# A shared sample search and denser key logits in a one-core hybrid decoder step

## The reference

```
x = x + 0.5 * swiglu(rms_norm(x)) ; h = rms_norm(x)
u, q, k, v, qi, ki, wi, gates = h @ w_in, split, normed, rotated
sample scores: sum over index heads of wi * relu(qi . ki) over 4096 cached + 8 new keys
idx = top 256 keys per query; logits = q . k[idx]; att = softmax(logits) @ v[idx]
x = x + (gate_c * conv(u) + gate_a * (att @ w_aout)) @ w_o
x = x + 0.5 * swiglu(rms_norm(x))
```

## Time and profile before

| | |
|---|---|
| median of the runs | 1529.44 us |
| profiled execution | 1525.64 us |
| its span | 1523.2 us |
| PE busy | 1428.6 us (94%) |
| VectorE busy | 1070.5 us (70%) |
| POOL busy | 587.3 us (39%) |
| ACT busy | 512.5 us (34%) |
| granted clock, mean | 0.98 |

### The profile page before, as it was taken

The page is one execution under the profiler, slowest core; times in us unless marked ns, Lnnn a source line. Parts: engine busy times, 40 slices in busy tenths (PEclk is TensorE's granted clock), DMA queues, the critical chain, the costliest instruction groups (busy, mean ns, idle before and its releaser), DMA issues. The chain is left out here.

```text
span 1523.2 us, 20730 instructions
## 1 busy us (share of the span) xinstructions
PE 1428.6 (94%) x8219; PEld 1123.1 (74%) x8219; DVE 1070.5 (70%) x1640; ACT 512.5 (34%) x776; POOL 587.3 (39%) x415
## 2 busy tenths in 40 slices
PE   4998999989989999999889898999998999999998
PEld 2333688867878875436666565679998999999998
DVE  1257798998826898999996997667669756664221
ACT  2333422123632231121112233453365444453111
POOL 2000564444338755544335675223203553420000
PEclk8998999999999999999999999999999999999999
DMA  9995363222227888879438875532422223312222
GB/s 345 391 380 205 99 98 105 89 81 69 81 77 246 286 258 291 279 215 314 152 102 272 265 229 175 170 132 75 134 87 69 87 83 109 99 50 74 84 87 87
DMA packets 156929, 248.75 MB, mean 163 GB/s; under 512 B 11965, under 2 KB 104909, under 8 KB 156571
## 3 DMA queue, kind: packets, MB, share of 16 engines
q1 hardware_dynamic: 131742, 164.22, 33.3%
q0 software_dynamic: 23104, 76.16, 15.9%
q10 hardware_dynamic: 1989, 7.07, 1.2%
HBM read 237.58 MB, written 10.20 MB: 163 GB/s over the span
## 5 line engine op out<-in xcount | busy, mean ns | idle before, releaser
L2749 POOL TENSOR_TENSOR w_lo<-w_raw,w_hi 128x1024 fp32r<-128x1024 f32 x65 | 168.2, 2589 | 243.9 <-ACT w_hi L1331 243.7
L695 PE MATMUL ps<-bh,wqr 128*128 128x288 f32 x936 | 205.3, 295 | 4.2 <-DVE wqr L1922 2.0
L1331 ACT ACTIVATE w_hi<-w_raw 128x1024 fp32r<-128x1024 f32 (+1 forms) x88 | 91.4, 1039 | 251.9 <-PE ps L646 181.4
L2816 POOL DMA_INDIRECT kv<-cache_v,idxT x128 | 136.6, 1068 | 100.1 <-PE ps L1109 50.6
L2804 POOL DMA_INDIRECT kv<-cache_k,idxT x128 | 138.5, 1082 | 86.1 <-DVE kprod L2442 53.9
L695 PEld LDWEIGHTS ps<-bh,wqr 128*128 128x128 f32 x936 | 155.5, 188 | 5.1 <-DVE wqr L1922 3.9
L646 PE MATMUL ps<-h_hi,w_hi 128*128 128x512 f32 x352 | 138.6, 394 | 1.2 <-POOL w_lo L2749 1.2
L646 PE MATMUL ps<-h_hi,w_lo 128*128 128x512 f32 x352 | 137.1, 390 | 0.0
L646 PE MATMUL ps<-h_lo,w_hi 128*128 128x512 f32 x352 | 137.0, 389 | 0.0
L711 PE MATMUL ps<-a_hi,wqr 128*128 128x288 f32 x704 | 122.6, 295 | 0.0
L1094 PE MATMUL ps<-h,wn 128*128 128x288 f32 x448 | 114.3, 412 | 8.8 <-DVE U_p L2269 3.7
(11 more groups left out here) (499 smaller groups left out, 3156.8 us busy)
## 6 DMA issues: line engine op xcount, KB each, us to landing
w_raw<-w_ffn_in SPq DMA_DIRECT2D x56, 512.0 KB, 12.4
wq<-w_ffn_in SPq DMA_DIRECT2D x40, 512.0 KB, 3.6
wn<-w_in SPq DMA_DIRECT2D x36, 512.0 KB
qb<-q_scratch SPq DMA_DIRECT2D x64, 256.0 KB
ring<-w_ffn_in SPq DMA_DIRECT2D x28, 512.0 KB
w_raw<-w_ffn_out SPq DMA_DIRECT2D x24, 512.0 KB, 9.6
wq<-w_ffn_out SPq DMA_DIRECT2D x20, 512.0 KB
ring<-w_ffn_out SPq DMA_DIRECT2D x14, 512.0 KB
```

Source lines behind the costliest of these rows:

```text
L695: mm = pe.matmul(ps[:, bank + m, 0:HALF], w[:, k, m * P:(m + 1) * P], b[:, j, k, :], start=(j in (0, 1, 5) and k == 0 and fst), stop=(k == ...
L1331: act.activation(w_hi[:, slot, 0:n], w_raw[:, slot, 0:n], ACT.Copy).then_inc(S_("hi_ready"), 1)
L2749: pool.tensor_tensor(w_lo[:, slot, 0:n], w_raw[:, slot, 0:n], w_hi[:, slot, 0:n].bitcast(F32), ALU.subtract)\
L2816: pool.indirect_dma_start(kv[:, V_SLOT[j % 3] + a // 2, a % 2, :], None, rows[1], bass.IndirectOffsetOnAxis(ap=idxT[:, j % 2, t:t + 1], ax ...
```

## The change

It has four parts. **The search is shared:** VectorE counts the first 1184 columns of `S`, and ACT counts the other 928 by Sign with an accumulator (`tally`, between its high parts, L1595 of the new kernel). VectorE joins the two counts with one more instruction, and a new function `next_up` follows the 31 steps: one more count over all columns and an addition of one where needed. **The work behind it stands earlier on PE:** the ranks are turned after unit 25 (28 before), the ends spread after 26, the one-hot products follow units 31 to 38, the rows unit 39 (43 before). **Key logits:** places begin at 41 (45 before), with two in every odd unit from 47 to 57; 34 tokens instead of 26 have a place ahead of `UA`. **Low parts:** those of units 45, 48, 51 and 54 are made by VectorE.

```
+        CUT = 1184
-        ROWS_AT = 43
+        ROWS_AT = 39
-        KEYS = [v for v in range(45, 59)] + ...
+        KEYS = [v for v in range(41, 59) for n in range(1 + (v >= 46 and v % 2))] + [v for v in range(59, 67)] + [67, 67]
+        SHARED = (45, 48, 51, 54)
-            return max(KEYS[n - KV] + 3, gather_after(n - 1) + 1)
+            return max(KEYS[n - KV] + 3, gather_after(n - 1) + (n % 3 > 0))
 # PE
-                        if (i, j) == (5, 0):
+                        if (i, j) == (4, 1):
                             ranks_turn()
-                        if (i, j) == (5, 1):
+                        if (i, j) == (4, 2):
                             ends_spread()
-                        if (6, 2) <= (i, j) <= (7, 3):
-                            onehots(4 * i + j - 26)
+                        if (5, 3) <= (i, j) <= (7, 2):
+                            onehots(4 * i + j - 23)
 # ACT
+            def tally(n):
+                for r in range(counted[0], counted[0] + n):
+                    act.wait_ge(S_("choice_step"), r + 2)
+                    act.activation(EQ[:, CUT:], S[:, CUT:], ACT.Sign, scale=-1.0, bias=ismall[:, 2:3].bitcast(F32), accum_out=cnts[:, 1:2]).then_inc(S_("scored"), 1)
...
+                    if i > i0 and i < 4:
+                        high_part(i - 1)
+                        tally(1)
                     hi(b + 2)
                     if i == 0:
                         qk_sample_evac()
+                    if i < 4:
+                        tally(2)
+                    hi(b + 3)
                     act.wait_ge(S_("unit_used"), b + 4)
                     (silu)
-                    hi(b + 3)
+                    if i < 4:
+                        tally(2)
                     hi(b + 4)
+                    if i < 4:
+                        tally(1)
                 for n in range(1, 9 if t < 2 else 8):
                     hi(out_unit(t) + n)
+                    if t == 0 and n < 6:
+                        tally((1, 2, 2, 1, 2)[n - 1])
 # VectorE, a step of the search
-                    lk(count(x_.bitcast(F32), ALU.is_ge, cnts[:, 0:1]))
-                    both(cnts[:, 1:2], cnts[:, 0:1])
+                    link(dve.tensor_scalar(EQ[:, 0:CUT], S[:, 0:CUT], x_.bitcast(F32), 0.0, ALU.is_ge, ALU.add, accum_out=cnts[:, 0:1]))
+                    dve.wait_ge(S_("scored"), 16 + i + 1)
+                    settle()
+                    lk(dve.scalar_tensor_tensor(out=cnts[:, 2:3], in0=cnts[:, 1:2], scalar=-0.5, in1=cnts[:, 0:1], op0=ALU.mult, op1=ALU.add))
+                    both(cnts[:, 3:4], cnts[:, 2:3])
...
-            search(27, 29)
-            out_add(0, 2)
-            search(29, 31)
-            out_add(0, 3)
+            search(28, 31)
+            out_add(0, 1)
+            next_up()
             lk(dve.tensor_tensor(x_, cur, flip, ALU.bitwise_xor))
...
             (cnts[:, 5:6], L2338)
+            out_add(0, 2)
             (selection, L2339, L2340)
+            out_add(0, 3)
             (second scan, L2343)
...
             onehot(0)
+            prod(5)
+            onehot(1)
             low_part(5)
-            onehot(1)
             onehot(2)
 # VectorE, the keys' loop; POOL, the loop of the low parts
+                if v + 2 in SHARED:
+                    dve.wait_ge(S_("lo_ready"), v + 4)
+                if in_unit(10) <= v + 2 < UA or v + 2 in SHARED:
                     split_lo(v + 2, v % 2, usize(v + 2))
...
+                if u - 1 in SHARED:
+                    pool.wait_ge(S_("lo_ready"), u + 2)
+                if u not in SHARED:
+                    lo(u)
```

More of the change, by code:

```diff
@@ L1532, in _ @@
                 rb = (relu_a, relu_b, relu_c, relu_d)[n // 2 % 4]
-                act.activation(rb[:, n % 2, :, :], ps[:, 2 * (n % 2):2 * (n % 2) + 2, :], ACT.Relu).then_inc(S_("relu_ready"), 1)
+                act.activation(rb[:, n % 2, :, :], ps[:, 2 * (n % 2):2 * (n % 2) + 2, :], ACT.Relu).then_inc(S_("scored"), 1)
                 if n == 6:
@@ L1598, in _ @@
                         qk_sample_evac()
-                    if i > i0:
+                    if i > i0 and i >= 4:
                         high_part(i - 1)
[L1601 to L1604, removed]
+                    if i < 4:
+                        tally(2)
+                    if i in (6, 7):
+                        weigh(4 * i - 22)
+                    hi(b + 3)
                     act.wait_ge(S_("unit_used"), b + 4)
@@ L1619, in _ @@
                         high_part(i1 - 1)
-                    if t == 1 and n in (1, 3):
-                        weigh(6 + n // 2)
+                    if t == 0 and n < 6:
+                        tally((1, 2, 2, 1, 2)[n - 1])
                     if t == 2 and n in (4, 6, 7):
@@ L2355, in _ @@
             dve.wait_ge(S_("ranks_taken"), 4)
-            low_part(4)
             lk(dve.tensor_scalar(tmpi[:, :, :], RTi[:, :, :], 4, None, ALU.arith_shift_right))
@@ L2370, in _ @@
                 if c == 0:
-                    prod(5)
+                    low_part(4)
             dve.sem_inc(S_("ranks_taken"), 1)
@@ L2402, in _ @@
             onehot(0)
+            prod(5)
+            onehot(1)
             low_part(5)
-            onehot(1)
             onehot(2)
-            prod(6)
-            onehot(3)
-            low_part(6)
-            onehot(4)
-            onehot(5)
             dve.wait_ge(S_("ends_done"), 2)
@@ L2416, in _ @@
             settle()
-            prod(7)
+            onehot(3)
+            onehot(4)
+            onehot(5)
+            prod(6)
             take_own(0)
-            low_part(7)
             onehot(6)
+            low_part(6)
             onehot(7)
@@ L2424, in _ @@
                               nb[:, :].unsqueeze(1).to_broadcast([NS, H, NS]), ALU.add).then_inc(S_("X_ready"), 1)
-            out_add(1, 0)
             take_own(1)
@@ L2458, in _ @@
                     prod(10)
-                if in_unit(10) <= v + 2 < UA:
+                if v + 2 in SHARED:
+                    dve.wait_ge(S_("lo_ready"), v + 4)
+                if in_unit(10) <= v + 2 < UA or v + 2 in SHARED:
                     split_lo(v + 2, v % 2, usize(v + 2))
-                for cg in range(1, 4):
-                    if v == max(out_end(1, cg), ROWS_AT + 1):
+                if v == ROWS_AT + 1:
+                    prod(7)
+                    low_part(7)
+                for cg in range(4):
+                    if v == out_end(1, cg):
                         out_add(1, cg)
```

70 lines of the change are left out of this document (41 added, 29 removed).

## The result

The changed kernel takes 1544.39 us (median of 7 runs, 1541.86 to 1552.73); the kernel before took 1528.35 in the same session. The ratio is 1.0116, 95% interval 1.0088 to 1.0143: slower. The forecast was 1541, slower, with a range up to 1551. The profiled execution has a span of 1540.3 us against 1523.2, 17.1 more. The total came out near the forecast, in part by luck: two of its terms were wrong by 7 and by 3.5 us, in opposite directions.

A forecast was written before the change was run, and what follows sets the result against it. PE was taken as the bound nearly everywhere. Terms 2.8 + 5.5 + 2.9 + 2.5 - 2.0 = +11.7 on 1525.64 gave 1537.3, and with 3.8 for the median 1541 us; range 1521 to 1551, the forecast case's own 1531 to 1548.

The forecast's parts named there:

- The first tallies: Units 3 and 4: ACT's high parts stand behind tallies, 1.4 us later at each; +2.8, bounds -0.9 to +4.5.
- ACT's stream: Rival: tallies of 1.5 us instead of 1.15 delay units, 1548; chance 0.12 together with none of the saving.
- The shared port: Two-input VectorE instructions and POOL low parts exclude each other; a unit's first join waits 1.4 us, its second does not.
- The search's end and the ranks: Units 24 to 25: search ends at 286.9, ranks at 325.5, PE waits 12.7 for 7.2; +5.5, bounds -2.5 to +11.
- a shift of 2.8: The lateness from the first tallies, +2.8 us, carried to later units, so unit 25 ends at 312.8.
- my signs of being wrong: `CUM` ends less than 8 us after unit 25, or over 6 us of PE's waits go behind unit 67.
- The one-hots: One-hot products: waits of 3.0 at the first and 5.8 at the third, none at the seventh; +2.9, bounds -6 to +6.
- The keys: Units 46 to 58: VectorE and POOL both full, a late VectorE low part near unit 58; +2.5, bounds 0 and +8.
- Behind unit 67: VectorE has 8 logits fewer, the 0.76 wait and most of the 1.80 go; -2.0, bounds -6.2 and 0.
- The rivals: Short chain 1521, 0.17; VectorE's work behind unit 67 1534, 0.16; ACT's stream 1548 or none of the saving, 0.12.
- The short chain: Rival: joins, `next_up` and copies meet no low part, ranks come at 315.7; -8, 1521; chance 0.17.
- The search could end where it did: Rival: VectorE's half plus waiting costs what was saved, ranks some 12 us later; over 1548; chance 0.12 with ACT's stream.

The follow-up runs named there:

- onehot_order: The changed kernel with `low_part(5)` behind the third set of one-hots, not ahead of it; ratio to the kernel before 1.0023.
- paced_gathers: The changed kernel with POOL, behind its low parts, starting each key token's gather no earlier than its logit's unit; ratio to the kernel before 1.0028, chip 13.
- combined: Kernel before plus shared search, units 3 and 4 high parts ahead of first tallies, one-tensor-operand join and XOR, `out_add(0, 2)` and `out_add(0, 3)` earlier; ratio 0.9964.
- after_again: The changed kernel as it is, run again on chip 4; ratio to the kernel before 1.0060.

## Why the forecast was right, and where not

The total is 5.4 us over the forecast. Of that 1.5 stands ahead of unit 0, where nothing changed; 7.0 too little for the keys and 3.5 too much for ranks and one-hots offset each other in part. That is luck, and the mechanism of the largest term, the keys, was not the one worked out.

*The first tallies (+2.8, bounds -0.9 to +4.5).* Right: 0.95 and 1.2 at units 3 and 4, where 1.4 each was worked out, and 0.9 at unit 8, which was not foreseen. A tally takes 1.07 and 0.19 us (1.15 between starts was expected), so ACT's stream did not break.

*The shared port.* Right in kind, shown by the two forms of the join. Of 31 joins only six were held over a microsecond, not one in two: I laid them over the low parts by one unit's pattern.

*The search's end and the ranks (+5.5).* The chain was right: counted from the same unit the search ended within 0.2 us of the 286.9 worked out, and PE waited for `xT` at unit 24 (4.5, forecast 5.6) and then for `CUM`. The ranks were mis-sized: `CUM` was ready at 324.08, with the start of units 4.7 later, so 3.3 earlier than 325.5 at a shift of 2.8. Of these 2.7 are `next_up`, which took 4.4 us (289.90 to 294.27) and not 7.1: none of its small ones was held. The one held was the XOR behind it (L2361, 2.05), which I had counted as free; in return of the two copies only one was held (2.21), and from that XOR on the chain took 29.8 for 30.2. PE's wait was 2.2, not 7.1, while unit 24 cost 2.6 us of slow matmuls, a term missing from my sum here though I had it for the one-hots; nor had I seen that the slow turned ranks of before (3.63 us, now 1.97) would go. By unit 30, which has ranks and ends behind it in both kernels, the stage had cost 1.0 us, not 5.5. One of my signs of being wrong was that `CUM` ends less than 8 us after unit 25. It ended 2.1 after it; without the waits ahead, as the sum reckoned (314.7), 9.4 after it. The sign was badly put, for the forecast itself left only 7.1 there.

*The one-hots (+2.9).* Right in both waits: 2.77 for 3.0 and 5.70 for 5.8, and none at the seventh. From unit 30 to 47 the cost was 4.0, since the products behind both waits were slow (3.39 and 3.60 for 1.96) and I had 1.0 for one. onehot_order showed the reason given for the third, `low_part(5)` behind ACT's high part. This one place is worth 8 us at unit 47.

*The keys (+2.5, bounds 0 and +8).* Wrong, outside its own bounds: 9.5. The step that failed is what comes late there. I took a late low part of VectorE and priced that. The low part was late because ACT had PE's signal for unit 57 only 9.0 us after the unit's end; VectorE stood idle for 7.1 us before it made it. The wait of 4.97 and 1.7 of slow matmuls in unit 59 are 6.7 of the 9.5; the other 2.8, and the 3.4 of paced_gathers, are near the 2.5. Nothing in the sum stood for such a signal, though the kernel before shows one, 1.5 us late with 0.5 us to spare. Of the six traces with 26 tokens ahead of unit 67 and no pacing only combined waited there (3.86); of the four with 34 tokens three waited 3.4 to 5.0 and one 0.7. But two of the six and none of the four are of chip 13, where nothing waits; so the traces make it likely that density favours the wait, no pair of runs on one chip shows it, and combined shows that it is not needed for it. Why the signal comes late beside a run of gathers, and on one chip and not on another, stays open, and so does whether taking the profile has a part in it.

*Behind unit 67 (-2.0).* The number is right, the reason only partly. PE is 19.1 us behind the kernel before at 573 and 13.5 at 783 (the waits answering to the earlier trace rows: 0.76 went, 3.66 became 1.96, but 1.80 stayed), and 19 behind again at 866. The largest piece of what is lost there is ACT's wait for a mix unit:

```profile
826.26 4.15 PE L1094 MATMUL ps<-h,wn 128*128 128x288 f32 x16
```

```profile
834.32 1.19 ACT L1682 ACTIVATE sgb<-ps 128x576 f32<-128x576 f32 x2 [9.78 <-remote]
```

```profile
835.56 5.83 PE L1094 MATMUL ps<-h,wn 128*128 128x288 f32 x16 [3.14 <-ACT sgb L1682]
```

The matmuls end at 830.41 and PE's semaphore is recorded at 834.30: a late signal again, of 3.9 us. On the chip of after_again 10 us are won by 878 and all given back by 993, in waits of 3.1 and 6.1 for the turned softmax, the second of them behind a signal of PE that came 7.7 us late. Late signals stand in this stage of the kernel before as well. Whether they are why the stage from 850 to 1000 gives back what the stages before it win is not settled: no experiment changed it alone.

*The rivals.* None of them alone. The short chain was half true at the ranks. "The search could end where it did" was false: it ended 10 us earlier.

## What to carry to other kernels

When a chain is shortened and its users are moved up with it, each instruction between them must be placed anew: the shared search alone was a small gain, and one low part left ahead of a set of one-hot cuts made a loss of 8 us behind it. Before adding work to a stage, look at its tightest hand-over in the trace and how late it can afford to be; here it was PE to ACT to VectorE, with 0.5 us to spare. When the profile shows a wait behind a transfer, check when the transfer was through before blaming it. And run both kernels on one chip before calling a wait cured. Removing one wait on the port that VectorE and GpSimd share moved it to the next instruction with two operands, or onto GpSimd's own work, each time that it was tried here.

## What the runs showed of the hardware

A per-partition scalar operand from SBUF in place of a second tensor operand kept the join free of GpSimd: 31 joins of 0.21 us against 0.16 to 2.74. Behind the wait of 4.5 us ahead of unit 24 twelve matmuls took 0.63 us and more instead of 0.39, 2.6 us beside the wait itself. The granted clock of that stretch (the number behind the engines) lies between its levels of 1.2 and 2.4 GHz:

```profile
309.00:316.00 7.00, 7.00 (x23) 5.52 (x22) 6.85 (x9) 0.00 (x0) 0.00 (x0) 0.67 0.24 75
```

PE's semaphore signal reached ACT 5.5 to 9.0 us after the last matmul of unit 57 in five of eight traces outside chip 13 with a run of gathers beside it, amid the gathers or 1 to 3 us behind the last of them, and let ACT go on within 0.1 us in all four traces of chip 13. And two traces of the kernel before, from two sessions, differed by up to 12 us behind unit 59 while the weight stream up to it agreed to 0.2 us.
